# Longer head groups in the expert-list stage: fourteen u tiles, sixteen stripes, and sums in three steps

## The reference

```python
q = (xt @ w_q).reshape(n, PEER_HEADS, 2, PEER_HALF)            # 8 heads, 2 halves of 128
s = jnp.einsum('nhpd,hpkd->nhpk', q, subkeys)                  # 128 keys per half
s_top, i_top = lax.top_k(s, 16)                                # the two lists
cand = s_top[:, :, 0, :, None] + s_top[:, :, 1, None, :]       # 256 candidates
best, sel = lax.top_k(cand.reshape(n, 8, 256), 16)             # 16 experts per head
eidx = i_top[...,0] * 128 + i_top[...,1]                       # at sel: one of 16384 experts
gate = softmax(best)
a = gelu(einsum('ted,td->te', u[eidx], x)); out = einsum('te,ted->td', gate * a, v[eidx])
```

## Time and profile before

| | |
|---|---|
| median of 3 runs | 4668.0 us (4661.43 to 4668.24) |
| profiled execution, its own time | 4653.4 us |
| its span | 4651.9 us |
| TensorE busy | 4258.3 us (92%) |
| VectorE busy | 2677.6 us (58%) |
| ScalarE busy | 1249.7 us (27%) |
| GpSimd busy | 1727.8 us (37%) |
| mean granted TensorE clock | 0.953 of full speed |

### The profile page before, as it was taken

The page is one execution under the profiler, slowest core; times in us unless marked ns, Lnnn a source line. Parts: engine busy times, 40 slices in busy tenths (PEclk is TensorE's granted clock), DMA queues, the critical chain, the costliest instruction groups (busy, mean ns, idle before and its releaser), DMA issues. The chain is left out here.

```text
span 4651.9 us, 76801 instructions
## 1 busy us (share of the span) xinstructions
PE 4258.3 (92%) x28688; PEld 4148.1 (89%) x28688; DVE 2677.6 (58%) x3552; ACT 1249.7 (27%) x1625; POOL 1727.8 (37%) x1305
## 2 busy tenths in 40 slices
PE   5999999999698898979999988898886999999997
PEld 5999999999465798979999988888886999999997
DVE  4222112111322452246889999666666888888887
ACT  4111133332212221132323222222222333233232
POOL 0000000000111000002555545778785766766772
PEclk8999999999698999989999999999997999999998
DMA  4822333332476443135666656898887999999996
GB/s 159 312 81 82 126 111 105 107 111 86 142 261 254 139 136 122 63 135 195 240 233 232 219 198 241 322 340 314 323 309 292 373 355 363 357 359 358 359 354 259
DMA packets 279276, 1061.58 MB, mean 228 GB/s; under 512 B 43634, under 2 KB 94194, under 8 KB 225970
## 3 DMA queue, kind: packets, MB, share of 16 engines
q1 hardware_dynamic: 165490, 522.72, 31.9%
q0 software_dynamic: 93728, 510.53, 29.1%
q10 hardware_dynamic: 19936, 26.78, 1.6%
HBM read 977.47 MB, written 81.33 MB: 228 GB/s over the span
## 5 line engine op out<-in xcount | busy, mean ns | idle before, releaser
L139 DVE TENSOR_TENSOR w_lo<-w_raw,w_hi 128x1024 fp32r<-128x1024 f32 x498 | 599.6, 1228 | 1020.1 <-ACT w_hi L130 1010.2
L130 ACT ACTIVATE w_hi<-w_raw 128x1024 fp32r<-128x1024 f32 x498 | 518.9, 1058 | 1226.7 <-PE acc L167 756.5
L1307 POOL DMA_INDIRECT routes_scratch<-gate_sums,route x384 | 552.0, 1438 | 275.8 <-DVE gate_sums L1462 120.9
L167 PE MATMUL acc<-x_hi,w_hi 128*128 128x288 f32 x2592 | 552.3, 295 | 18.0 <-DVE w_lo L139 18.0
L167 PE MATMUL acc<-x_lo,w_hi 128*128 128x288 f32 x2592 | 551.5, 294 | 0.0
L167 PE MATMUL acc<-x_hi,w_lo 128*128 128x288 f32 x2592 | 551.2, 294 | 0.0
L167 PE MATMUL acc<-h_hi,w_hi 128*128 128x384 f32 (+1 forms) x1280 | 409.7, 336 | 85.6 <-DVE w_lo L139 85.4
L167 PE MATMUL acc<-h_hi,w_hi_peeru 128*128 128x384 f32 (+1 forms) x1280 | 409.4, 336 | 36.7 <-DVE w_lo_peeru L139 36.7
L167 PEld LDWEIGHTS acc<-x_hi,w_hi 128*128 128x128 f32 x2592 | 416.5, 189 | 18.7 <-DVE w_lo L139 15.1
L167 PEld LDWEIGHTS acc<-x_lo,w_hi 128*128 128x128 f32 x2592 | 416.7, 189 | 0.0
L167 PEld LDWEIGHTS acc<-x_hi,w_lo 128*128 128x128 f32 x2592 | 416.3, 189 | 0.0
(11 more groups left out here) (309 smaller groups left out, 8557.5 us busy)
## 6 DMA issues: line engine op xcount, KB each, us to landing
w_raw<-in_w_peer_u SPq DMA_DIRECT2D x256, 512.0 KB, 3.9
w_raw<-in_w_peer_v SPq DMA_DIRECT2D x256, 512.0 KB, 3.7
w_raw<-in_w_gate SPq DMA_DIRECT2D x96, 512.0 KB, 3.9
w_raw<-in_w_z SPq DMA_DIRECT2D x66, 512.0 KB, 3.3
k_ring<-in_cache_k SPq DMA_DIRECT2D x64, 512.0 KB, 5.1
v_ring<-in_cache_v POOLq DMA_DIRECT2D x64, 512.0 KB, 6.6
routes_scratch<-zero POOLq DMA_DIRECT2D x8, 3072.0 KB, 49.2
activations_scratch<-a_out ACTq DMA_DIRECT2D x128, 192.0 KB
```

Of the source, the lines that this page charges most:

```text
L130: nc.scalar.activation(slot(q, j)[0], raw[:, j % 4, :], ACT.Copy).then_inc(q["hi"], 1)
L139: nc.vector.tensor_tensor(lo, raw[:, j % 4, :], hi.bitcast(F32), ALU.subtract).then_inc(q["lo"], 1)
L167: last = nc.tensor.matmul(dst, l_, r_[:, cc, c0:c0 + cn], start=(cc == first and p_ == 0), stop=(cc == last_c and p_ == 2))
L1307: pool.indirect_dma_start(route_dram, bass.IndirectOffsetOnAxis(ap=route[:, b, n:n + 1], axis=0), gsum[:, h % SUMS, b - 1, n % PTOP:n % PT ...
```

## The change

The group grows from 10 to 16 stripes: a head's two q stripes come with fourteen u tiles, and 16 tiles are left over behind the eighth head in place of 64. The steps are spread over it: `choose` takes one block per stripe (five steps in place of three), `candidates`, `unpack` and `look_up0` have stripes of their own, and `add_same` becomes three steps of up to three earlier heads each (`sums0`, `sums1`, `sums2`) in stripes 18, 19 and 20 of the head. `s_head` is given at the end of `sums2`. Head 0 is done in stripe 12 as before, head h in stripe 16 h + 20: head 7 in stripe 132.

`dots_by` starts at stripe 16 with one dot per stripe up to 38, then gives three in two stripes up to 134 and five in two behind that. The first dot of head h now falls into stripe 16 h + 24 (h from 2 on). `scatters_before` starts each head with 4 scatters and puts three more before every further gather, so that the head's 48 are through before its sixteenth gather; the other eight gathers of the head have none between them. The data, the number of every kind of instruction on TensorE, ScalarE, GpSimd and the DMA queues, and the arithmetic are unchanged.

```diff
--- before.py
+++ after.py
@@ -1230,7 +1230,7 @@
         s_gat = [sem(f"u_row_gathered{k}") for k in range(3)]
         s_used, s_sct, s_gel = sem("u_row_used"), sem("gates_scattered"), sem("gelu_done")
 
-        GROUP = 10
+        GROUP = 16
         U_IN = GROUP - 2
 
         def stripe(s):
@@ -1240,26 +1240,29 @@
                 return ("q", 2 * g + r) if r < 2 else ("u", U_IN * g + r - 2)
             return "u", s - NQ
 
-        HEAD_STEPS = {4: ("list0",), 5: ("list1",), 6: ("list2",), 7: ("list3",), 8: ("list4",), 9: ("candidates", "choose0"),
-                      10: ("choose1",), 11: ("choose2", "shift"), 12: ("unpack", "look_up0"), 13: ("look_up1",), 14: ("number", "weigh"), 15: ("add_same",)}
-        FIRST_STEPS = {4: ("list0", "list1"), 5: ("list2", "list3"), 6: ("list4", "candidates"), 7: ("choose0",), 8: ("choose1",),
-                       9: ("choose2", "shift"), 10: ("unpack", "look_up0"), 11: ("look_up1", "number"), 12: ("weigh",)}
+        HEAD_STEPS = {4: ("list0",), 5: ("list1",), 6: ("list2",), 7: ("list3",), 8: ("list4",), 9: ("candidates",),
+                      10: ("choose0",), 11: ("choose1",), 12: ("choose2",), 13: ("choose3",), 14: ("choose4", "shift"), 15: ("unpack",),
+                      16: ("look_up0",), 17: ("look_up1", "number"), 18: ("weigh", "sums0"), 19: ("sums1",), 20: ("sums2",)}
+        FIRST_STEPS = {4: ("list0", "list1"), 5: ("list2", "list3"), 6: ("list4", "candidates"), 7: ("choose0", "choose1"),
+                       8: ("choose2", "choose3"), 9: ("choose4", "shift"), 10: ("unpack", "look_up0"), 11: ("look_up1", "number"), 12: ("weigh",)}
         plan = {}
         for h in range(PH):
             for r, names in (HEAD_STEPS if h else FIRST_STEPS).items():
                 for name in names:
                     plan.setdefault(GROUP * h + r, []).append((h, name))
         exp_at = {s + 1: h for s in plan for h, name in plan[s] if name == "shift"}
-        move_at = {s + 1: h for s in plan for h, name in plan[s] if name == ("add_same" if h else "weigh")}
-        LAST_STEP = GROUP * (PH - 1) + 14
+        move_at = {s + 1: h for s in plan for h, name in plan[s] if name == ("sums2" if h else "weigh")}
+        LAST_STEP = GROUP * (PH - 1) + 20
 
         def dots_by(s):
 
-            return 0 if s < 14 else min(NGAT, s - 13 if s < LAST_STEP else LAST_STEP - 13 + 2 * (s - LAST_STEP))
+            if s < 16:
+                return 0
+            return s - 15 if s <= 38 else min(NGAT, 23 + 3 * (min(s, 134) - 38) // 2 + 5 * max(0, s - 134) // 2)
 
         def scatters_before(q):
 
-            return 4 + 3 * q if q < 70 else min(NSCT, 214 + (q - 70) * 170 // 120)
+            return 48 * (q // 24) + min(48, 4 + 3 * (q % 24))
 
         with nc.Block() as block:
             @block.sync
@@ -1423,8 +1426,8 @@
                                                  top[:, :, 0, :].unsqueeze(3).to_broadcast([P, NBLK, PTOP, PTOP]),
                                                  top[:, :, 1, :].unsqueeze(2).to_broadcast([P, NBLK, PTOP, PTOP]), ALU.add))
 
-                def choose(blocks):
-                    link(sixteen([(cand[:, b, :], rest_c[:, n, :], best[:, b, :], sel[:, b, :]) for n, b in enumerate(blocks)]))
+                def choose(b):
+                    link(sixteen([(cand[:, b, :], rest_c[:, b % 2, :], best[:, b, :], sel[:, b, :])]))
 
                 def shift():
                     nc.vector.tensor_tensor(ebest[:], best[:], best[:, :, 0:1].to_broadcast([P, NBLK, PTOP]), ALU.subtract).then_inc(s_eb, 1)
@@ -1465,10 +1468,14 @@
                     else:
                         link(last)
 
-                def add_same(h):
-
-                    dve.wait_ge(s_lst, NBLK * (h + 1) + (h < PH - 1))
-                    for h0 in range(0, h, 3):
+                def add_same(h, part_no):
+
+                    h0 = 3 * part_no
+                    if h0 == 0 and h < PH - 1:
+                        dve.wait_ge(s_lst, NBLK * (h + 1))
+                    if h0 < h:
+                        if part_no == 2 and h < PH - 1:
+                            dve.wait_ge(s_lst, NBLK * (h + 1) + 1)
                         n = min(3, h - h0) * PTOP
                         c0 = h0 * PTOP
                         link(nc.vector.tensor_tensor(same[:, :, :, 0:n], eid_f[:, 1:4, :].unsqueeze(3).to_broadcast([P, 3, PTOP, n]),
@@ -1476,10 +1483,9 @@
                         link(nc.vector.tensor_tensor(same[:, :, :, 0:n], same[:, :, :, 0:n],
                                                      gate[:, 1:4, c0:c0 + n].unsqueeze(2).to_broadcast([P, 3, PTOP, n]), ALU.mult))
                         link(nc.vector.reduce_sum(psum_[:], same[:, :, :, 0:n], AX.X))
-                        last = nc.vector.tensor_tensor(gsum[:, h % SUMS], gsum[:, h % SUMS], psum_[:], ALU.add)
-                        if h0 + 3 < h:
-                            link(last)
-                    last.then_inc(s_head, 1)
+                        link(nc.vector.tensor_tensor(gsum[:, h % SUMS], gsum[:, h % SUMS], psum_[:], ALU.add))
+                    if part_no == 2:
+                        dve.sem_inc(s_head, 1)
 
                 def step(h, name):
                     if name.startswith("list"):
@@ -1487,7 +1493,7 @@
                     elif name == "candidates":
                         candidates()
                     elif name.startswith("choose"):
-                        choose(((0, 1), (2, 3), (4,))[int(name[6:])])
+                        choose(int(name[6:]))
                     elif name == "shift":
                         shift()
                     elif name == "unpack":
@@ -1499,7 +1505,7 @@
                     elif name == "weigh":
                         weigh(h)
                     else:
-                        add_same(h)
+                        add_same(h, int(name[4:]))
 
                 def dot(q):
                     i, r = divmod(q, 3)
```

## The result

The changed kernel takes 4685.55 us (median of 20 runs, 4665.90 to 4693.15) against 4664.48 (20 runs, 4652.94 to 4682.06). The ratio is 1.0038 with an interval of 1.0028 to 1.0047, so it is slower by 0.38%, 17.7 us by the ratio (the two medians lie 21.1 apart). The forecast was slower by 43 us. Direction and range hold; the size is under half, by either figure.

The account below looks back on a forecast made before the run. The prediction took the expert-list stage's second part to be bound by GpSimd's indirect DMAs, held beside VectorE's dots. Losses of 20 + 102 + 71 = 193 us against 150 gave +43 us, 4711 us, range 4630 to 4770 us.

Parts of the forecast that it names:

- Step (1): Sums spread over three stripes: 20 us lost in place of 45, chiefly at head 7 (12) and head 6 (3).
- Step (2): Rows of six heads, dotted between stripes 40 and 132: GpSimd falls short, 17 us lost per head, 102 in all.
- Step (3): Behind stripe 132: the last head's scatters and gathers take 174 us against 92.4 and 10.6 of cover, 71 lost.
- the heavy rival: GpSimd at its late price, 2.11 us per instruction, everywhere: 280 us lost, 4798 us; chance 0.12 above 4760.
- The cheap end: The last head's 64 instructions at the first part's price of 1.62 us: 104 us, and 40 lost in place of 71.
- Step (4): Everything else, such as instruction counts, TensorE's work, ScalarE, loads and the stages behind: no cost.
- the "over 198" of the text: Sign in the profile: VectorE's waits for gathered rows sum to over 198 us.
- 8 us and more: Sign in the profile: behind stripe 135 TensorE waits this long per stripe.
- The text's sign against term (3): The end's loss, put at 71 us, falls if the last 11 stripes take under 110 us.
- The first rival: GpSimd keeps up at nearly 1.27 us per instruction, deciding below 1.5: 35 us lost for 150, 4553 us; chance 0.12.

Follow-up runs that it names:

- two_each: The changed kernel with two scatters ahead of each gather in place of three: 4599.97 us, 0.9856 of the kernel before.
- last_unscattered: The changed kernel without the 48 scatters of the eighth head: 4646.09 us, 0.9957 of the kernel before.
- end_paced: The changed kernel with its dots at three in two stripes to the end, not five in two from stripe 134: 4689.12 us, 1.0050.
- row_sums: The changed kernel with each dot replaced by a one-input sum over the gathered row: 4705.04 us, 1.0084 of the kernel before.
- row_sums_two: The changed kernel with one-input row sums for the dots and two scatters ahead of each gather in place of three: 4561.98 us, 0.9774.

## Why the prediction was half right

**Step (1), the sums: right.** 20 us forecast, about 22 found by the drains: 13 at head 7 (stripes 131 to 133 take 18.60, 9.63 and 10.02 us), 4 at head 6, and 5 at head 5, which was put at nothing. (For head 7 the text's own figures, 58.8 - 42 less a lead of 6, give 10.8 us and not the 12 that it took.) Alone, in groups of ten, this part gives 16 us.

**Step (2), dots and scatters of six heads: right in cause and sum, 95 us for 102.** The stripes 32 to 47, 48 to 63 and so on up to 127, in which the rows of heads 1 to 6 are dotted, lose 9.2, 15.0, 14.6, 16.3, 18.4 and 17.9 us (sums left out), and stripes 128 to 130 another 3.7. The forecast had 17 for each; the first lies near half of that and the last, with the 3.7, a quarter above it, so that the sum came out nearer than single heads did. The working, 21.3 us for two stripes with twelve instructions, is what the trace has: VectorE's share of stripes 106 and 107 takes 22.3 us. Two details were off. The list stripes lose nothing, since the lead and the rows already in the ring cover them, and all of it falls into the `choose` stripes; and the first waits come at 2445 us, in stripe 44. GpSimd's mean under the heads is 1.56 us, forecast 1.55. From stripe 1 to stripe 99 no wait of TensorE is over 6.9 us. `two_each` shows that the bunching is the cause: it takes 72 of the 117 us away and changes nothing but GpSimd's order.

**Step (3), the end: the mechanism right, the term mis-sized, 49 us for 71.** The forecast said 64 instructions at 2.11 us, 135 us, and 31 + 8 us behind them. GpSimd in the changed kernel, a late gather, the first scatter of head 8, its sixteenth gather and the last one of all:

```profile
3363.19 1.68 POOL L1322 DMA_INDIRECT ring<-in_peer_u,expert_sample  x1 [1.67 <-DVE ring L1514]
3365.17 3.11 POOL L1310 DMA_INDIRECT routes_scratch<-gate_sums,route  x1 [0.30 <-issue]
...
3476.56 0.98 POOL L1322 DMA_INDIRECT ring<-in_peer_u,eidx  x1 [0.30 <-issue]
...
3504.36 0.94 POOL L1322 DMA_INDIRECT ring<-in_peer_u,expert_sample  x1 [1.93 <-DVE ring L1514]
```

The 64 take 3477.54 - 3365.17 = 112.4 us, **1.76 us each and not 2.11**; from there to the gelu are 34.7 us and not 39; and 6.9 us that were not forecast lie between the drain of stripe 132 and the first scatter, because two older gathers stand ahead of it in GpSimd's list and one waits for its ring slot. 154 us against the forecast 174, less the same 92.4 and 10.6, is 51, of which 1.6 belong to the sums.

The price is the step that failed. 2.11 was the pitch of the second part of before, with all its gaps, where VectorE was busy 386 of 584 us, 66%. Two things are wrong with it here. The gaps were not all the queue's 0.30 us: they came to 0.44 us per instruction, since GpSimd there also waited 22.5 us for ring slots and 11.9 us for landed scatters, so 2.11 was not its capacity. At the end of the changed kernel the gaps between the 64 are 0.30 us each, which makes 0.14 of the 0.35 us. The other 0.2 us come from fewer being held: 40 of the 64 took 1.06 us or less against 119 of 275 before, while the held ones last as long as ever, 2.25 against 2.23 us. VectorE is busy 75 of 139 us there, 54%, since it stands waiting for rows, and the groups of the window from 3368 us show instructions of 1.43 to 1.69 us:

```profile
L1310 POOL DMA_INDIRECT routes_scratch<-gate_sums,route x48 | 68.7, 1432 | 14.6 <-issue 14.6
L1322 POOL DMA_INDIRECT ring<-in_peer_u,eidx x16 | 25.7, 1605 | 13.9 <-DVE ring L1514 9.9 <-issue 4.0
L1322 POOL DMA_INDIRECT ring<-in_peer_u,expert_sample x8 | 13.5, 1685 | 4.1 <-issue 2.1 <-DVE ring L1514 1.9
```

The text had the reason at hand, as the case against the heavy rival: a waiting VectorE frees GpSimd. It did not apply it to its own term. The cheap end that it gave, 64 x 1.62 and 40 us, is nearer than the one it took. Nearer still is the price of its own step (2), for the same three scatters to a gather: 21.3/12 = 1.775 us, which makes 114 us for the 64 where 112.4 were measured. That the scatters make the end is shown by `last_unscattered`; that VectorE's order doesn't, by `end_paced`.

**Step (4), nothing else: right.** The stages around the block differ by 1.4 us between the two profiles; the single items of the step were not tested one by one.

The sum: 22 + 95 + 49 = 166 against 150 is +16, where 193 against 150 gave +43; 22 of the 27 us too much are step (3), 7 step (2), and -2 step (1). The sum of VectorE's waits came out at 192, a little under the "over 198" of the text, and TensorE's waits in stripes 137 to 142 are 4.7 to 8.3 us and not 8 and more. The text's sign against term (3), the last 11 stripes in under 110 us, could not catch the fault: they took 149.4 us. The first rival would have needed under 1.5 us per instruction; under the heads it was 1.56. The Trainium skill's rule behind it ("SBUF — State Buffer", "Who interferes with whom"), that a `tensor_tensor` doesn't delay descriptor generation, would give that; the time that it gives didn't come about here, since 130 of 132 indirect DMAs begun inside a dot were held until its end, and with one-input reductions of the same length none was. (The dots are `scalar_tensor_tensor`; for a `tensor_tensor` there is the example of the prediction, a gather that ended 0.85 us behind a split.) Whether the dots hold the writing of descriptors or GpSimd's reading of indices from SBUF, no run tells apart.

## What to carry to other kernels

When work of an in-order engine feeds another, count its instructions per step of the pipeline and spread them evenly: here two in place of three scatters per gather is worth 1.8%, and turns a slower kernel into one 1.4% faster than before. A list that is finished later takes its consumers' cover with it; price what stands behind it against what is left of the stage. And price a contended instruction at the load that its neighbour will have in the new place, since an engine that waits doesn't disturb: 1.76 us here where 2.11 had been assumed.

## What the runs showed of the hardware

- An indirect DMA holds GpSimd 0.97 us beside idle or one-input VectorE work, also beside a `TENSOR_REDUCE` of 2.28 us (`row_sums`, 173 cases), and until some 0.86 us behind the end of a `SCALAR_TENSOR_TENSOR` within which it began (2.99 us at 2598.30; 130 of 132 cases). The gathers' mean moved from 1.91 to 1.15 us with nothing but the form of the dots.
- Where GpSimd starts indirect DMAs every 1.28 us in long rows, TensorE stood idle for up to 1.62 us between two matmuls with no wait named (2.2 us at most), though not at every such row: 4705 us (`row_sums`) against 4562 (`row_sums_two`) for the same work in another order. The cause is open. In `row_sums` a faster GpSimd was thus worth nothing until its list was thinned out.
